# Latent attention over a prompt: value columns as the stationary operand for two heads at once, and GpSimd dividing the probabilities

## The chip, the core and the metric

The kernel runs on one core of one Trainium2 chip. The metric is the device time of one execution in microseconds (us); lower is better. A core has a matrix engine (TensorE, "PE" in the profile, with its weight loads shown apart as "PEld"), a vector engine (VectorE, "DVE"), an activation engine (ScalarE, "ACT"), a general engine (GpSimd, "POOL") and SyncE ("SP"), which only issues transfers. Each engine works through its own list of instructions in order and waits on semaphores for the others. Matrix products go from SBUF to PSUM, an accumulator memory of eight banks of 512 fp32 columns on 128 partitions.

## The reference

One decoder layer is computed for a prompt of 1024 tokens and for one new token of each of eight requests. It has dilated attention, latent attention (MLA), gates, cross attention to a memory, and a feed-forward part. The change is in the latent attention of the prompt alone:

```python
def mla_prompt(qc, rows):            # qc: 8 heads, rows: latent 256 | rotated key 32
    vals = rows[..., :MLA_KV_LORA]
    def block(b):                    # 128 queries at a time
        logits = einsum('bqhc,bkc->bhqk', qb, rows) * MLA_SCALE
        logits = where(kpos[None, :] <= t[:, None], logits, -inf)
        p = softmax(logits, axis=-1)
        return einsum('bhqk,bkc->bqhc', p, vals)
...
o_b = einsum('bshc,chv->bshv', o_lat, p['w_uv'])   # 64 value columns per head
```

Everything is fp32, and the scores are causal.

## The kernel before

The program is a sequence of stages with a barrier of all engines between them. The stage in question is the second block of `stage_mla`. It finds the queries in `qnT` and `qrT`, the normed latent rows in `rowT`, the rotated keys in `krT`, and the values of all heads, already multiplied by `w_uv`, as `vtok` (128 tokens of a key tile on the partitions, 64 columns for each head). Keys of a pair of heads are made by `keys` as a product with `w_uk`, in two halves of 512 tokens, and ScalarE copies them to `kh` (`key_copy`).

The work is cut into 64 units: 8 heads by 8 query tiles of 128 tokens. Unit (h, t) has t + 1 key tiles, so its cost grows along a head. A unit goes through these steps:

1. `score` (line 1022, TensorE): one or two products of up to 512 key columns into one of two double banks of PSUM. It waits until the unit two places before has been exponentiated (`probs`).
2. `front` (VectorE): adds the causal mask to the diagonal tile (line 1131), takes the row maximum (line 1135), and scales it by `-MLA_SCALE` (line 1136).
3. `exp` (line 1090, ScalarE): writes the unnormalised probabilities to `mla_pr`, and their sums to a column of `mla_stat`.
4. the reciprocal of the sums (line 1153, VectorE).
5. `turn` (line 1034, TensorE): transposes each 128 by 128 tile of probabilities, four into PSUM bank 4 and the others into bank 5.
6. The copies of the turned tiles to `mla_pt`: VectorE copies the first four (line 1158), ScalarE the others (line 1107).
7. `apply` (line 1046, TensorE): the turned probabilities are the weights and the 64 value columns of the head are streamed, so that the output has tokens on the partitions.
8. `normalise` (line 1143, VectorE): multiplies the 64 output columns by the reciprocal and puts them in `mla_otok`.

Units follow each other with t running inside h. TensorE's list has `score(u + 1)`, `turn(u)`, `apply(u - 1)`; VectorE's has `front(u + 1)`, the reciprocal, the copy and `normalise(u - 1)`. After the last unit TensorE turns `mla_otok` (line 1068), and VectorE and ScalarE copy it to `obT`, heads on the partitions, which the next product needs.

GpSimd has side work in this stage: it copies the queries of heads 1 to 7 to `qh` (`queries`, lines 1175 and 1177), makes the row numbers of the cache pages for the following stage, lays out the queries of that stage (lines 1192 and 1195, four rounds of 16 small copies), and at its end starts the gather of the first cache pages (line 1200, `first_rows`). None of this stands in the way of a unit, except the queries of the next head. SyncE has 24 transfers in this stage that move the cache windows to the outputs, from one place of HBM to another.

The following stage reads 32 units of cache pages by gathers from GpSimd (line 1266), and VectorE begins it by transposing the first page (line 1375).

Of the kernel before, what the change touches and what calls it, by code (L numbers as in the profile page):

```python
# [24 lines left out]
P = 128  # L25
# [599 lines left out]
def stage_mla(nc, ins, outs, top, sem, sb, ps, mats, ones, gq, gkv, latT, lat, obT, part_scr, s_copy, end_phase,  # L625
# [328 lines left out]
    with ExitStack() as st:  # L954
        HR = NOPE + ROPE
        qh = sb(st, "mla_qh", [P, 2, SEQ])
        kh = sb(st, "mla_kh", [P, 2, SEQ])
# [8 lines left out]
        qh_set, q0_set, kr_set, pool_own = sem("qh_set"), sem("q0_set"), sem("kr_set"), sem("mla_pool_own")  # L966
# [4 lines left out]
        applied, normed = sem("mla_applied"), sem("mla_normed")  # L971
        o_turned, ob_copied = sem("o_turned"), [sem("ob_copied_v"), sem("ob_copied_a")]
        tiles = [(h, t) for h in range(H) for t in range(QT)]
        N_U = len(tiles)


# [5 lines left out]
        with nc.Block() as block:  # L982
# [15 lines left out]
            def _(pe):  # L998
# [8 lines left out]
                def score(u):  # L1007
                    h, t = tiles[u]
                    if t == 0:
# [4 lines left out]
                        if h == 0:  # L1014
                            pe.wait_ge(kr_set, 3)
                    if t in (0, 4):
                        pe.wait_ge(k_copied, 4 * (h // 2) + h % 2 + (3 if t else 1))
                    if u >= 2:
                        pe.wait_ge(probs, u - 1)
                    for lo in range(0, (t + 1) * P, 512):  # L1020
                        n = min(512, (t + 1) * P - lo)
                        last = nc.tensor.matmul(ps[:, 2 * (u % 2) + lo // 512, 0:n], qh[spans[h % 2], h % 2, t * P:(t + 1) * P],
                                                kh[spans[h % 2], h % 2, lo:lo + n], start=True, stop=True)
                    last.then_inc(scored, 1)

                def turn(u):
                    t = tiles[u][1]
                    pe.wait_ge(probs, u + 1)
                    for hi in range(t // 4 + 1):
# [3 lines left out]
                        for k in range(4 * hi, min(4 * hi + 4, t + 1)):  # L1033
                            last = nc.tensor.transpose(ps[:, 4 + hi, (k - 4 * hi) * P:(k - 4 * hi + 1) * P],
                                                       pr[:, u % 2, k * P:(k + 1) * P], ident)
# [17 lines left out]
                for u, (h, t) in enumerate(tiles):  # L1053
                    if u + 1 < N_U:
                        score(u + 1)
                    turn(u)
                    if u >= 1:
                        apply(u - 1)
                    if t in (3, 7) and h % 2 and h + 1 < H:
                        keys((h + 1) // 2, t // 4)  # L1060
                apply(N_U - 1)

                for t in range(QT):
                    pe.wait_ge(normed, (H - 1) * QT + t + 1)
                    if t >= 4:
                        pe.wait_ge(ob_copied[t % 2], (t - 2) // 2)
                    for c in range(4):
                        last = nc.tensor.transpose(ps[:, t % 4, c * P:(c + 1) * P], otok[:, t, c * P:(c + 1) * P], ident)
                    last.then_inc(o_turned, 1)

            @block.scalar
            def _(act):
                def key_copy(p, half, odd):
                    act.wait_ge(k_made, 2 * p + half + 1)
                    if p:
                        act.wait_ge(scored, (2 * p - 1 + odd) * QT)
# [1821 lines left out]
```

## Time and profile before

| what | value |
|---|---|
| runs | 2304.74, 2307.99, 2309.16 us; median 2307.99 us |
| profiled execution | span 2303.0 us from its first to its last instruction; no other time of that execution is listed, and the median of the runs is 5.0 us above this span |
| TensorE busy | 2133.7 us, 93% of the span |
| VectorE, ScalarE, GpSimd busy | 1036.3, 518.8 and 83.4 us |
| mean granted TensorE clock | 0.959 |
| the stage of the change | about 577 to 778 us of the span |

The profile counts an engine as busy while an instruction of it runs. Matrix products are pipelined and overlap, so the sum of their durations is larger than the busy time. "Idle before" is time in which an engine waited, and the arrow names what ended the wait. A PE instruction count is that of passes: an fp32 product is issued as two passes, each with its own weight load, and a transpose as one.

### The profile page before, as it was taken

Reading aid. Unit: us, or ns where it says so; the run is one execution under the profiler, and the core shown is the slowest. Engines: PE = TensorE matmul, PEld = TensorE weight load, DVE = VectorE, ACT = ScalarE, POOL = GpSimd, SP = SyncE. Lnnn points to the kernel's source line nnn. Section 1 sums busy time; section 2 is a strip of 40 time slices with the busy share of each in tenths; the row PEclk is TensorE's granted clock in tenths of the full one; section 3 lists DMA queues with packets and bytes.
Section 4 is the critical chain, followed back from the end, with each engine's and each line's share of the span. In section 5 each row is a group of like instructions: output and inputs, shape, how many; then the busy total and the mean of one; then the engine's idle time right before and its main releaser. Section 6 shows DMA issues by size and latency. Waiting matters only on the chain. (4 is left out here: it accounts for less than half of the span.)

```text
span 2303.0 us, 40007 instructions
## 1 busy us (share of the span) xinstructions
PE 2133.7 (93%) x17452; PEld 1864.2 (81%) x17452; DVE 1036.3 (45%) x1338; ACT 518.8 (23%) x959; POOL 83.4 (4%) x139
## 2 busy tenths in 40 slices
PE   8999967789899889988999999789999999999998
PEld 7999945564677545557988898679999999999998
DVE  5222244644666678972222335675323323422424
ACT  4000004430434223331111223352101101101111
POOL 0000000001400011100000000000000000000000
PEclk9999977889999899998999999899999999999999
DMA  6113132020895389965211130301111111111122
GB/s 210 47 46 128 28 111 83 2 60 21 286 327 196 142 304 335 350 236 171 73 41 47 53 119 10 110 19 37 55 46 38 55 46 38 47 55 38 47 59 79
DMA packets 178911, 241.74 MB, mean 105 GB/s; under 512 B 27211, under 2 KB 165427, under 8 KB 173412
## 3 DMA queue, kind: packets, MB, share of 16 engines
q1 hardware_dynamic: 172792, 155.80, 22.0%
q0 software_dynamic: 5904, 83.95, 9.8%
q8 instruction: 94, 1.54, 0.3%
q10 hardware_dynamic: 92, 0.20, 0.0%
q14 instruction: 29, 0.24, 0.0%
HBM read 217.20 MB, written 66.72 MB: 123 GB/s over the span
## 5 line engine op out<-in xcount | busy, mean ns | idle before, releaser
L2530 PE MATMUL ps<-xn_hi,mlp_w_hi 128*128 128x344 f32 x768 | 163.3, 321 | 2.6 <-issue 2.0
L2530 PE MATMUL ps<-xn_hi,mlp_w_lo 128*128 128x344 f32 x768 | 162.4, 319 | 2.9 <-issue 2.9
L2530 PE MATMUL ps<-u_lo,mlp_w_hi 128*128 128x344 f32 x768 | 163.0, 320 | 0.0
L2530 PE MATMUL ps<-u_hi,mlp_w_hi 128*128 128x344 f32 x768 | 162.9, 320 | 0.0
L1282 PE MATMUL ps<-mla_rt,q_now 32*32 32x256 f32 x4608 | 147.3, 388 | 16.8 <-issue 9.9
L2530 PE MATMUL ps<-mlp_xn_lo,mlp_w_hi 128*128 128x344 f32 x768 | 162.8, 320 | 0.0
L2530 PE MATMUL ps<-u_hi,mlp_w_lo 128*128 128x344 f32 x768 | 162.1, 319 | 0.0
L1282 PEld LDWEIGHTS ps<-mla_rt,q_now 32*32 32x32 f32 x4608 | 86.2, 107 | 65.1 <-issue 39.8
L1375 DVE STREAM_TRANSPOSE mla_rt<-qkvT 128x1536 f32<-128x1536 f32 x72 | 124.4, 1758 | 30.5 <-DMA qkvT<-in_cache_mla,page_rows 27.8
L1693 DVE TENSOR_TENSOR hT<-hT,ps 128x1032 f32<-128x1032 f32 x28 | 34.4, 1229 | 223.9 <-PE ps L2530 223.9
L2530 PE MATMUL ps<-xn_hi,gate_w_hi 128*128 128x344 f32 x576 | 128.6, 332 | 6.5 <-DVE gates L2069 4.3
L2530 PEld LDWEIGHTS ps<-xn_hi,mlp_w_hi 128*128 128x128 f32 x768 | 128.7, 188 | 6.7 <-issue 5.6
L2530 PEld LDWEIGHTS ps<-u_lo,mlp_w_hi 128*128 128x128 f32 x768 | 130.0, 189 | 0.0
L2530 PEld LDWEIGHTS ps<-u_hi,mlp_w_hi 128*128 128x128 f32 x768 | 129.2, 188 | 0.0
L2530 PEld LDWEIGHTS ps<-xn_hi,mlp_w_lo 128*128 128x128 f32 x768 | 128.9, 188 | 0.0
L2530 PEld LDWEIGHTS ps<-mlp_xn_lo,mlp_w_hi 128*128 128x128 f32 x768 | 128.7, 188 | 0.0
L2530 PEld LDWEIGHTS ps<-u_hi,mlp_w_lo 128*128 128x128 f32 x768 | 127.9, 188 | 0.0
L2530 PE MATMUL ps<-xn_hi,win_hi 128*128 128x344 f32 x576 | 123.4, 322 | 4.1 <-DVE xn_lo L2794 4.1
L2530 PE MATMUL ps<-gates_xn_lo,gate_w_hi 128*128 128x344 f32 x576 | 123.6, 323 | 0.0
L2530 PE MATMUL ps<-xn_hi,gate_w_lo 128*128 128x344 f32 x576 | 123.2, 323 | 0.0
L2530 PE MATMUL ps<-xn_hi,win_lo 128*128 128x344 f32 x576 | 122.5, 321 | 0.0
L2530 PE MATMUL ps<-xn_lo,win_hi 128*128 128x344 f32 x576 | 122.5, 321 | 0.0
(407 smaller groups left out, 3438.4 us busy)
## 6 DMA issues: line engine op xcount, KB each, us to landing
out_s_dsa_w<-in_cache_dsa_w SPq DMA_DIRECT2D x8, 4094.0 KB, 81.7
oaT<-in_w_up SPq DMA_DIRECT2D x32, 512.0 KB, 4.1
oaT<-in_w_down SPq DMA_DIRECT2D x32, 512.0 KB, 4.0
obT<-in_w_in SPq DMA_DIRECT2D x23, 512.0 KB
gate_w<-in_w_in SPq DMA_DIRECT2D x16, 512.0 KB, 4.1
out_s_dsa_w<-in_cache_dsa_w SPq DMA_DIRECT2D x8, 1022.0 KB, 17.9
s_kv_tile<-in_cache_dsa_w SPq DMA_DIRECT2D x12, 512.0 KB, 5.3
x_scr<-qkvT SPq DMA_DIRECT2D x1, 4128.0 KB, 13.3
```

Of the source, the lines that this page charges most:

```text
L1282: last = nc.tensor.matmul(ps[32 * (JG * s + g):32 * (JG * s + g) + 32, i, 0:JN * SQ], q_now[SQ * i:SQ * i + SQ, s, c, :], rt[SQ * i:SQ * i ...
L1375: nc.vector.transpose(rt[:, k * n:(k + 1) * n], rows[v][:, :, k * n * SQ:(k + 1) * n * SQ].rearrange("p n (c f) -> p c n f", c=n)).then_in ...
L1693: nc.vector.tensor_tensor(h, h, banks(s), ALU.add).then_inc(drained[s], 1)
L2530: last = nc.tensor.matmul(out[:, t, 0:TC], w, x[:, k, t * TC:(t + 1) * TC], start=first, stop=stop)
```

## The change

The order of the units becomes: pairs of heads, then query tiles, then the two heads of the pair. `apply` is done once for a pair and a query tile. The 64 value columns of a head are now the weights, and the 128 by 128 turned probabilities are streamed; the even head uses the first 64 columns of the array and the odd head the last 64 (`tile_position`). The output has value columns on the partitions, in the layout of `obT`, and ScalarE copies it there. `mla_otok`, its transposes and its copies are gone.

The sums no longer lie on the partitions of the output. So GpSimd multiplies the probabilities by the reciprocals, in place, before they are turned, and `turn` waits for that (`normed`). The queries are multiplied by `-MLA_SCALE` when they are copied, the mask is subtracted, and the row minimum is taken, so that the step of line 1136 is gone. There are three buffers of probabilities in place of two, four of turned ones in place of two, and two sets of queries and keys. GpSimd's side work is spread among its multiplications: `queries` after units 3 and 5 of each block of 16 units, the second set of rotated keys and two clears after units 1 and 2, the page rows after unit 8, the four rounds of small copies (now `page_queries`) after units 17, 19, 21 and 23, and the gather of the first pages after the last unit.

```diff
-        pr = sb(st, "mla_pr", [P, 2, SEQ])
-        pt = sb(st, "mla_pt", [P, 2, QT, P])
-        otok = sb(st, "mla_otok", [P, QT, H * VD])
+        PRS, PTS = 3, 4
+        pr = lat_flat[:, 0:PRS * SEQ].rearrange("p (s n) -> p s n", s=PRS)
+        pt = sb(st, "mla_pt", [P, PTS, QT, P])
-        tiles = [(h, t) for h in range(H) for t in range(QT)]
+        tiles = [(2 * p + o, t) for p in range(H // 2) for t in range(QT) for o in range(2)]
+        PU = 2 * QT
...
                 def turn(u):
                     t = tiles[u][1]
-                    pe.wait_ge(probs, u + 1)
+                    pe.wait_ge(normed, u + 1)
...
-                def apply(u):
-                    h, t = tiles[u]
-                    pe.wait_ge(pt_copied[0], u + 1)
+                def apply(n):
+                    h, t = tiles[2 * n]
+                    pe.wait_ge(pt_copied[0], 2 * n + 2)
                     if t >= 4:
-                        pe.wait_ge(pt_copied[1], his(u + 1))
-                    if u >= 1:
-                        pe.wait_ge(normed, u)
+                        pe.wait_ge(pt_copied[1], his(2 * n + 2))
+                    if n:
+                        pe.wait_ge(o_copied, n)
                     for k in range(t + 1):
-                        last = nc.tensor.matmul(ps[:, 6, 0:VD], pt[:, u % 2, k, :], vtok[:, k, h * VD:(h + 1) * VD],
-                                                start=(k == 0), stop=(k == t))
+                        for o in range(2):
+                            last = nc.tensor.matmul(ps[VD * o:VD * o + VD, 6, 0:P],
+                                                    vtok[:, k, (h + o) * VD:(h + o + 1) * VD],
+                                                    pt[:, (2 * n + o) % PTS, k, :], start=(k == 0), stop=(k == t),
+                                                    tile_position=(0, VD * o), skip_group_check=True)
                     last.then_inc(applied, 1)
...
+                score(1)
+                for u in range(N_U + 2):
+                    if 1 <= u <= N_U:
+                        turn(u - 1)
+                    if u + 2 < N_U:
+                        score(u + 2)
+                    if u % 2 and u >= 3:
+                        apply((u - 3) // 2)
+                    if u % PU in (4, 10) and u // PU + 1 < H // 2:
+                        keys(u // PU + 1, 0 if u % PU == 4 else 1)
...
-                nc.scalar.activation(qh[0:NOPE, 0, :], qnT[0:NOPE, 0, 0:SEQ], ACT.Copy).then_inc(q0_set, 1)
+                nc.scalar.activation(qh[0:NOPE, 0, 0, :], qnT[0:NOPE, 0, 0:SEQ], ACT.Copy, scale=-MLA_SCALE).then_inc(q0_set, 1)
...
+                for u in range(N_U + 3):
+                    if u % 2 == 0 and u >= 4:
+                        n = (u - 4) // 2
+                        h, t = tiles[2 * n]
+                        act.wait_ge(applied, n + 1)
+                        nc.scalar.activation(obT[:, h // 2, t * P:(t + 1) * P], ps[:, 6, 0:P],
+                                             ACT.Copy).then_inc(o_copied, 1)
                     if u + 1 < N_U:
                         exp(u + 1)
...
-                    link(nc.vector.tensor_tensor(diag, diag, mats[:, C_CAUSAL:C_CAUSAL + P], ALU.add))
+                    link(nc.vector.tensor_tensor(diag, diag, mats[:, C_CAUSAL:C_CAUSAL + P], ALU.subtract))
...
-                    link(nc.vector.tensor_reduce(stat[:, u % 4, 0:1], src, AX_X, ALU.max))
-                    nc.vector.tensor_scalar(stat[:, u % 4, 1:2], stat[:, u % 4, 0:1], -MLA_SCALE, None,
-                                            ALU.mult).then_inc(maxed, 1)
+                    nc.vector.tensor_reduce(stat[:, u % 4, 0:1], src, AX_X, ALU.min).then_inc(maxed, 1)
-                def normalise(u):
-                    h, t = tiles[u]
-                    dve.wait_ge(applied, u + 1)
-                    dve.wait_ge(inverted, u + 1)
-                    nc.vector.tensor_scalar(otok[:, t, h * VD:(h + 1) * VD], ps[:, 6, 0:VD], stat[:, u % 4, 3:4], None,
-                                            ALU.mult).then_inc(normed, 1)
...
+                for u in range(N_U + 1):
                     if u + 1 < N_U:
                         front(u + 1)
+                    if u < N_U:
+                        dve.wait_ge(probs, u + 1)
+                        nc.vector.reciprocal(stat[:, u % 4, 3:4], stat[:, u % 4, 2:3]).then_inc(inverted, 1)
                     if u >= 1:
+                        nk = min(tiles[u - 1][1] + 1, 4)
+                        dve.wait_ge(turned[0], u)
+                        if (u - 1) // 2 >= 2:
+                            dve.wait_ge(applied, (u - 1) // 2 - 1)
+                        nc.vector.tensor_copy(pt[:, (u - 1) % PTS, 0:nk, :].rearrange("p k n -> p (k n)"), ps[:, 4, 0:nk * P]
+                                              ).then_inc(pt_copied[0], 1)
...
+                def normalise(u):
+                    n = (tiles[u][1] + 1) * P
+                    pool.wait_ge(inverted, u + 1)
+                    nc.gpsimd.tensor_scalar(pr[:, u % PRS, 0:n], pr[:, u % PRS, 0:n], stat[:, u % 4, 3:4], None,
+                                            ALU.mult).then_inc(normed, 1)
+                    pool.wait_ge(normed, u + 1)
...
+                for u in range(N_U):
+                    normalise(u)
+                    if u == 1:
+                        for s in range(2):
+                            nc.gpsimd.tensor_copy(kh[ropes[s], 1, s, :], krT[ropes[s], 0:SEQ]).then_inc(kr_set[1], 1)
+                            pool.wait_ge(kr_set[1], s + 1)
+                    if u == 2:
+                        nc.gpsimd.memset(kh[0:ROPE, 1, 1, :], 0.0).then_inc(kr_set[1], 1)
+                        pool.wait_ge(kr_set[1], 3)
+                        link(nc.gpsimd.memset(qh[0:ROPE, 1, 1, :], 0.0))
+                    if u % PU in (3, 5) and 2 * (u // PU + 1) < H:
+                        queries(2 * (u // PU + 1) + (u % PU - 3) // 2)
+                    if u == 8:
...
+                    if PU <= u < PU + 8 and u % 2:
+                        page_queries((u - PU) // 2)
                 pool.wait_ge(q0_set, 2)
                 pool.indirect_dma_start(first_rows[:], None, cache_rows,
```

## Rows read from the trace of the kernel before

**Rows 1.** Page: busy time of each engine, whole span.
```profile
PE 2133.7 (93%) x17452; PEld 1864.2 (81%) x17452; DVE 1036.3 (45%) x1338; ACT 518.8 (23%) x959; POOL 83.4 (4%) x139
```

**Rows 2.** Windows: length, PE, PEld, DVE, ACT, POOL busy, PE clock, DMA share, GB/s.
```profile
577.00:587.40 10.40, 6.39 (x12) 2.46 (x12) 5.56 (x10) 6.07 (x9) 6.47 (x12) 0.77 0.34 89
...
633.00:656.00 23.00, 21.68 (x143) 16.88 (x141) 16.40 (x50) 9.12 (x22) 2.06 (x2) 1.00 0.98 326
...
778.00:800.00 22.00, 15.30 (x315) 8.72 (x317) 15.37 (x15) 2.91 (x6) 2.82 (x3) 0.69 0.81 327
```

**Rows 3.** Waits in the stage, 576 to 780 us: total us, times, longest.
```profile
POOL mla_qh L1175 <- PE ps L1022: 100.9, 5, 21.3
...
DVE ps L1131 <- PE ps L1022: 38.0, 49, 2.9
...
DVE mla_otok L1143 <- PE ps L1046: 17.1, 16, 2.2
```

**Rows 4.** Groups of instructions by shape, 576 to 780 us: busy us, mean ns, idle before.
```profile
L1046 PE MATMUL ps<-qkvT,mla_pt 128*128 128x64 f32 x576 | 72.2, 271 | 0.5 <-DVE mla_otok L1143 0.5
...
L1158 DVE COPY mla_pt<-ps 128x512 f32<-128x512 f32 x40 | 27.0, 675 | 3.0 <-PE ps L1034 3.0
...
L1131 DVE TENSOR_TENSOR ps<-ps,mats 128x128 f32<-128x128 f32 x64 | 19.0, 297 | 38.0 <-PE ps L1022 38.0
L1143 DVE TENSOR_SCALAR mla_otok<-ps,mla_stat 128x64 f32<-128x64 f32 x64 | 17.7, 277 | 17.1 <-PE ps L1046 17.1
L1003 PE MATMUL ps<-qkvT 128*128 128x512 f32 x32 | 17.4, 669 | 6.2 <-PEq L693 4.9 <-ACT mla_kh L1077 1.3
...
L1153 DVE RECIPROCAL mla_stat<-mla_stat 128x1 f32<-128x1 f32 x64 | 9.8, 153 | 1.5 <-ACT mla_pr L1090 1.5
L1135 DVE TENSOR_REDUCE mla_stat<-ps 128x1 f32<-128x1024 f32 x8 | 9.8, 1225 | 0.3
...
L1090 ACT ACTIVATE mla_pr<-ps,mla_stat 128x1024 f32<-128x1024 f32 x8 | 8.9, 1113 | 18.0 <-DVE mla_stat L1136 18.0
...
L1135 DVE TENSOR_REDUCE mla_stat<-ps 128x1 f32<-128x128 f32 x8 | 2.3, 292 | 0.3
...
L1158 DVE COPY mla_pt<-ps 128x128 f32<-128x128 f32 x8 | 2.2, 274 | 0.2 <-PE ps L1034 0.2
```

**Rows 5.** Timeline of PE in the earlier dilated attention: start, us, instructions.
```profile
399.69 1.09 PE L542 MATMUL ps<-obT,arena 128*64 128x128 f32 x16 [2.33 <-ACT obT L577]
```

**Rows 6.** GpSimd's groups by shape, whole span: busy us, mean ns.
```profile
L1192 POOL COPY latT<-qkvT 32x256 f32<-32x256 f32 x32 | 12.5, 390 | 2.0
...
L1195 POOL COPY latT<-qkvT 32x8 f32<-32x8 f32 x32 | 6.1, 190 | 1.9
L863 POOL TENSOR_TENSOR oaT<-oaT,obT 128x1024 f32<-128x1024 f32 x2 | 4.7, 2350 | 55.2 <-DVE obT L894 55.2
...
L1186 POOL TENSOR_SCALAR page_rows<-page_rows 128x32 int32<-128x32 int32 x1 | 0.3, 299 | 2.9 <-DMA page_rows<-in_page_table 2.9
```

**Rows 7.** Timeline of GpSimd in the stage: start, us, instruction.
```profile
578.57 1.38 POOL L1175 COPY mla_qh<-qkvT 64x1024 f32<-64x1024 f32 x1
...
649.28 1.03 POOL L1175 COPY mla_qh<-qkvT 64x1024 f32<-64x1024 f32 x1 [21.27 <-PE ps L1022]
...
719.32 1.04 POOL L1175 COPY mla_qh<-qkvT 64x1024 f32<-64x1024 f32 x1 [21.19 <-PE ps L1022]
```

**Rows 8.** Timeline of all engines at the stage's end and after it.
```profile
767.44 1.09 PE L1034 MATMUL ps<-mats,mla_pr 128*128 128x128 f32 x8 [1.03 <-ACT mla_pr L1090]
...
770.51 1.97 PE L1046 MATMUL ps<-qkvT,mla_pt 128*128 128x64 f32 x16 [0.47 <-DVE mla_otok L1143]
...
776.02 0.60 ACT L1115 ACTIVATE obT<-ps 128x512 f32<-128x512 f32 x1 [0.28 <-PE ps L1068]
778.36 2.67 SPq L1248 DMA_DIRECT2D qkvT<-out_s_mla_rows  x8
...
789.83 3.44 DVE L1375 STREAM_TRANSPOSE mla_rt<-qkvT 128x1536 f32<-128x1536 f32 x2 [6.02 <-DMA qkvT<-in_cache_mla,page_rows]
```

More of the change, by code:

```diff
@@ L1013, in score @@
                             pe.wait_ge(qh_set, h)
-                        if h == 0:
-                            pe.wait_ge(kr_set, 3)
+                        if o == 0 and p < 2:
+                            pe.wait_ge(kr_set[p], 3)
                     if t in (0, 4):
-                        pe.wait_ge(k_copied, 4 * (h // 2) + h % 2 + (3 if t else 1))
+                        pe.wait_ge(k_copied, 4 * p + (2 if t else 0) + o + 1)
                     if u >= 2:
@@ L1021, in score @@
                         n = min(512, (t + 1) * P - lo)
-                        last = nc.tensor.matmul(ps[:, 2 * (u % 2) + lo // 512, 0:n], qh[spans[h % 2], h % 2, t * P:(t + 1) * P],
-                                                kh[spans[h % 2], h % 2, lo:lo + n], start=True, stop=True)
+                        last = nc.tensor.matmul(ps[:, 2 * (u % 2) + lo // 512, 0:n],
+                                                qh[spans[o], p % 2, o, t * P:(t + 1) * P],
+                                                kh[spans[o], p % 2, o, lo:lo + n], start=True, stop=True)
                     last.then_inc(scored, 1)
@@ L1052, in _ @@
                 score(0)
[L1053 to L1069, printed above, removed]
+                score(1)
[8 more added lines that the diff above has]
+                        keys(u // PU + 1, 0 if u % PU == 4 else 1)
             @block.scalar
@@ L1074, in key_copy @@
                     act.wait_ge(k_made, 2 * p + half + 1)
-                    if p:
-                        act.wait_ge(scored, (2 * p - 1 + odd) * QT)
-                    nc.scalar.activation(kh[parts[odd], odd, half * 512:(half + 1) * 512], ps[parts[odd], 7, :],
+                    if p >= 2:
+                        act.wait_ge(scored, (p - 1) * PU)
+                    nc.scalar.activation(kh[parts[odd], p % 2, odd, half * 512:(half + 1) * 512], ps[parts[odd], 7, :],
                                          ACT.Copy).then_inc(k_copied, 1)
@@ L1082, in exp @@
                     act.wait_ge(maxed, u + 1)
-                    if u >= 2:
-                        act.wait_ge(turned[0], u - 1)
-                        if his(u - 1):
-                            act.wait_ge(turned[1], his(u - 1))
+                    if u >= PRS:
+                        act.wait_ge(turned[0], u - PRS + 1)
+                        if his(u - PRS + 1):
+                            act.wait_ge(turned[1], his(u - PRS + 1))
                     if u >= 4:
@@ L1196, in _ @@
                                                    qrT[ROPE * (h % 4):ROPE * (h % 4) + ROPE, h // 4, SEQ:T]))
-                for h in range(2, H):
-                    queries(h)
+                nc.gpsimd.iota(sub_row[:], pattern=[[0, 1]], base=0, channel_multiplier=1).then_inc(sub_made, 1)
+                link(nc.gpsimd.memset(qh[0:ROPE, 0, 1, :], 0.0))
+                queries(1)
+                for u in range(N_U):
[11 more added lines that the diff above has]
+                    if u == 8:
+                        pool.wait_ge(sub_masked, 1)
+                        pool.wait_ge(tab_in, 16 * UNIT)
+                        link(nc.gpsimd.tensor_scalar(row_of[:], row_of[:], SUB, None, ALU.mult))
+                        link(nc.gpsimd.tensor_tensor(row_of[:], row_of[:], sub(sub_row[:, 0:1], [0, NU]), ALU.add))
+                        link(nc.gpsimd.memset(qq[:, CB - 1], 0.0))
+                    if PU <= u < PU + 8 and u % 2:
+                        page_queries((u - PU) // 2)
                 pool.wait_ge(q0_set, 2)
```

85 lines of the change are left out of this document (31 added, 54 removed).

## The prediction

> **What bounds the kernel now.** The page comes first: TensorE is busy for 93% of the span and no other engine for half of it [rows 1]. That is an average over many stages, so the stage of the change has to be read alone. Its windows show a full head with TensorE busy 21.68 of 23.00 us at a granted clock of 1.00 (the 2.4 GHz level), VectorE 16.40, ScalarE 9.12 and GpSimd 2.06 [rows 2]. The waits agree: VectorE waited 38.0 us in all for scores and 17.1 us for `apply`, and GpSimd's query copies waited 100.9 us for scores, because GpSimd had nothing else to do [rows 3]. So TensorE sets the pace, and GpSimd is the engine with room. How long a head takes is read from GpSimd, whose query copy starts once for each head: at 649.28 and, three heads later, at 719.32, that is 23.35 us a head [rows 7]. With the busy share of the window (0.943), TensorE works 22.0 us of it.
>
> The transfers of the cache windows fill the DMA engines in the stage (share 0.98 [rows 2]), but no unit waits for one.
>
> **TensorE's part.** Before, the turned probabilities are weights and 64 columns are streamed. The last `apply` has 16 passes for the 8 key tiles of one head and takes 1.97 us [rows 8]. After, 64 columns are weights and 128 columns are streamed, in two halves of the array. That form stands in the trace already, in the dilated attention (line 542: 128 by 64 weights, 128 columns streamed, two heads side by side): 16 passes for 8 pairs of key tile and head take 1.09 us [rows 5]. All `apply` is 72.2 us [rows 4]; 72.2 x 1.09 / 1.97 = 39.9, so 32.3 us go, 4.0 a head, and TensorE's work becomes 18.0 us a head. Of this the keys are 17.4 / 8 = 2.2 [rows 4] and the rest is 15.8 / 36 = 0.44 for each key tile.
>
> VectorE loses its `normalise` (17.7 us [rows 4]) and the scaling of the maximum. What is left is mask 0.30, minimum 0.29 for one key tile to 1.23 for eight (0.13 more for each), reciprocal 0.15, copy 0.27 for one to 0.68 for four or more [rows 4]. For units of one to four key tiles that is 1.02, 1.28, 1.55 and 1.82, together 5.7 us, where TensorE needs 0.44 x 10 = 4.4. So VectorE sets the pace of the short units and a head gets 1.3 us longer; half of the key work (1.1) falls among short units, where it then costs nothing. In long units TensorE leads: 3.5 us for eight key tiles against VectorE's 2.4. Half of before's 1.35 us of waiting a head I leave in (0.7), since hand-overs remain. A head comes to 18.0 + 1.3 - 1.1 + 0.7 = 18.9, say 19.0: 4.35 less than now, 34.8 us for eight heads. ScalarE gets 32 copies of 128 columns from PSUM, none longer than the 0.60 us of a copy of 512 [rows 8], four a head beside 9.12 us of work [rows 2]: hidden as long as TensorE or VectorE leads.
>
> **GpSimd's multiplication.** The trace has no fp32 multiplication by a per-partition number on GpSimd, so it is bounded from both sides. A copy, one tensor in and one out, takes 0.390 us for 256 columns [rows 6] and 1.03 for 1024 [rows 7]: 0.83 ns a column and 0.18 us fixed. A sum of two tensors takes 2.35 us for 1024 [rows 6], 2.12 ns a column. The only `TENSOR_SCALAR`, on 32 integers, takes 0.299 us [rows 6], above a copy of that size, which warns a little. The multiplication has one tensor in and one out, so I take the copy's price and keep the sum's for the range. At the copy's price eight key tiles are 1.03 us; a head is 4608 x 0.83 ns + 8 x 0.18 = 5.3 us, far under 19.
>
> What it costs is latency in a ring: score, mask, minimum, reciprocal, multiplication, turn, and the score two units later (TensorE issues `turn(u - 1)` before `score(u + 2)`). For eight key tiles, four passes as long as those of line 1003 (17.4 / 32 = 0.54 [rows 4]), 0.30, 1.23, 0.15, 1.03 and 1.09 [rows 4, 7, 8] give 6.0 us for two units, 3.0 for one, under TensorE's 3.5. At 2.35 for the multiplication it is 3.65 a unit, over 3.5.
>
> The Trainium skill, in GPSIMD Engine Reference, section Engine selection, speaks against giving GpSimd elementwise work: about half of VectorE's speed for two inputs, though roughly line-rate for one. This trace agrees on the first (2.35 us against VectorE's 1.2 for a minimum of as many columns); for the second there is a copy's 0.83 ns a column, and no multiplication. By the slower rule the time would be that of the first rival, which is worked out from rows below.
>
> **GpSimd's side work, now in the way.** While GpSimd does something else, the next multiplication waits, then `turn`, and with it all of TensorE's list behind it (`score(u + 2)`, `apply`, keys). With three buffers of probabilities, ScalarE and VectorE run on for one or two units at most.
> - The four rounds of small copies took 12.5 + 6.1 us with 2.0 + 1.9 between them [rows 6], 22.5 us in all, and were hidden behind the first units. Now they stand after units 17, 19, 21 and 23, among units of two to four key tiles. From the end of multiplication 17 to the start of 24 GpSimd has 22.5, two `queries` (four copies of 1.03, 4.1) and six multiplications (2304 columns x 0.83 ns + 6 x 0.18 = 3.0): 29.6 us. Unhindered those seven steps are 2 x (1.28 + 1.55 + 1.82) + 0.44 x 5 = 11.5, with hand-overs 12. Loss 17.6 us.
> - Six blocks of about 2.1 us (two copies of 1.03, or clears of that size) after units 1, 2, 3, 5, 35 and 37. GpSimd's free time in such a unit is about 1.2 (1.02 to 1.82 less 0.29 to 0.61). Each loses some 0.9: 5 us. Bounds 0 and 12.
> - TensorE idles in the stretch of rounds, and the granted clock falls where it idles (a mean of 0.77 and 0.69 in the windows that begin with a wait at a barrier, 1.00 in the steady one [rows 2]). In the stretch that costs nothing; after it, 1 us.
> - The first pages' gather left right after the copies of 719.32 [rows 7] and was long in when the next stage began. Now it leaves after the last multiplication, some 6 us before that stage. The second page, asked for at the start of that stage, landed at 789.83 [rows 8], some 11 us later, so the first can be up to 5 us late. But VectorE then waited 6.02 us for the second page [rows 8], and that wait takes up the delay: 0 to 5, I take 1.
>
> **The end.** From the last exponential (turn at 767.44) to the last copy (776.02 + 0.60) are 9.2 us [rows 8]. After: reciprocal 0.15, multiplication 1.03, turn 1.09, copy 0.68, `apply` of two heads 2 x 1.09, copy at most 0.60: 5.7. Gain 3.5. Negating the queries and subtracting the mask cost nothing: the same instructions with another constant, the first before any unit.
>
> **Sum.** -34.8 + 17.6 + 5 + 1 + 1 - 3.5 = -13.7 us on a span of 2303.0. The median of the runs is 5.0 above that span; I keep the distance: 2308.0 - 13.7 = 2294.
>
> **The rivals.**
> 1. GpSimd multiplies at the two-input price (slower). The ring then binds, some 0.15 a unit (9.6 us); the six multiplications in the stretch take 3.0 more; each `queries`, now two multiplications of 1024 columns, takes 2.6 more, for two heads in the stretch (5.3) and four elsewhere (10.6). Together 28.5: 2322. It decides from 1.46 ns a column on, where the sum is zero. For it: the 0.299 us row. Against it: one input. Chance 0.17, a quarter of it ending within the bound of no change.
> 2. The two halves of the array don't run at once. `apply` then takes about what it took, -34.8 shrinks to about -5, and the time is 2324. Against it: line 542 [rows 5]. Chance 0.04.
> 3. The ring, not TensorE, sets the pace of long units too, through hand-overs that I have not counted: 20.5 us a head, 12 us more, 2306, no change. For it: six hand-overs in the ring and ScalarE's list, where the output copy stands before the next exponential. Against it: 3.0 against 3.5. Chance 0.15.
> 4. The rounds are hidden after all, if the stages around them have run ahead: 2294 - 17.6 = 2276. Against it: three buffers. Chance 0.08.
>
> **How the numbers follow.** The forecast keeps 0.56. A measurement of this kernel can tell 0.2%, 4.6 us, from no change. Faster holds the forecast, rival 4 and 0.3 of rival 3: 0.68. No change: most of rival 3 and a quarter of rival 1: 0.13. Slower: 0.19. The low end takes 0.7 less waiting a head (5.6) and blocks that cost nothing (5) and a little of rival 4: 2281. The high end goes 20 us up, to 1.74 ns a column: 2314. Inside the forecast alone, 2283 to 2303.
>
> **What would show it.** Line 542's price for the new `apply`; heads at 19 us where GpSimd has no side work (units 48 to 63); GpSimd busy without a break for some 30 us around units 17 to 24, with TensorE waiting for its multiplication; a multiplication of 1024 columns at 1.03 us. The forecast is wrong if that row is above 1.7 us, if the last 16 units don't get faster, or if the rounds' stretch shows no wait.

## The result, and the profile after

| | runs | median |
|---|---|---|
| before | 2304.74 to 2314.10 us (4) | 2308.57 us |
| after | 2336.36 to 2348.65 us (4) | 2343.34 us |

The ratio is 1.0154, with an interval of 1.0127 to 1.0181: the change made the kernel slower by 35 us, where 14 us faster were predicted. The profiled execution has a span of 2346.9 us (2303.0 before). The execution profiled before is the fastest of its four and the one profiled now the slowest, so these spans lie 43.9 us apart. Nearly all of that, 43.6 us, lies in the stage of the change: from ScalarE's first query copy to the first `q_now` of the next stage it took 200.9 us before and takes 244.5 us now.

First GpSimd's groups of the changed kernel in that stage, which answer to the copies of [rows 6, 7] (line, engine, operation, shapes, count, busy us, mean ns, idle before):

```profile
L1173 POOL TENSOR_SCALAR latT<-latT,mla_stat 128x1024 f32<-128x1024 f32 x8 | 22.7, 2843 | 3.1 <-DVE mla_stat L1146 2.8
...
L1163 POOL TENSOR_SCALAR mla_qh<-qkvT 64x1024 f32<-64x1024 f32 x7 | 19.7, 2809 | 0.6
L1165 POOL TENSOR_SCALAR mla_qh<-qkvT 32x1024 f32<-32x1024 f32 x7 | 19.3, 2762 | 0.6
...
L1180 POOL COPY latT<-qkvT 32x256 f32<-32x256 f32 x32 | 12.6, 393 | 2.0
...
L1173 POOL TENSOR_SCALAR latT<-latT,mla_stat 128x128 f32<-128x128 f32 x8 | 4.8, 603 | 10.5 <-DVE mla_stat L1146 10.2
```

The multiplication (line 1173) of 1024 columns takes 2.84 us where 1.03 was predicted. From 128 to 1024 columns that is (2843 - 603) / 896 = 2.5 ns a column. The queries (lines 1163 and 1165), copies of 1.03 before, have become the same kind of instruction and take 2.8 each, with 64 or 32 partitions alike. Copies cost what they did (0.393 us for 256 columns, 0.390 before).

TensorE's groups: the new `apply` (line 1048) has the price that line 542 had promised. The turn (line 1035) waited 57.2 us for the multiplication.

```profile
L1035 PE MATMUL ps<-mats,latT 128*128 128x128 f32 x288 | 49.0, 300 | 57.2 <-POOL latT L1173 57.2
L1048 PE MATMUL ps<-mla_pt,qkvT 128*64 128x128 f32 x576 | 40.1, 285 | 0.7 <-DVE mla_pt L1152 0.7
```

The waits of the stage (total us, times, longest): before, VectorE waited for TensorE for 38.0 and 17.1 us [rows 3]. Now TensorE waits for GpSimd's multiplication, and VectorE's copy of the turned tiles waits for TensorE's turn behind it.

```profile
...
PEld ps L1035 <- POOL latT L1173: 74.7, 39, 9.3
DVE mla_pt L1152 <- PE ps L1035: 73.7, 46, 9.2
PE ps L1035 <- POOL latT L1173: 57.2, 30, 9.1
```

The windows, from the first exponential of 1024 columns of one pair of heads to that of the next (columns as in [rows 2]): the second pair, the third, and the fourth, which makes no keys for a next one.

```profile
631.16:703.81 72.65, 44.89 (x273) 27.25 (x272) 27.08 (x66) 19.98 (x52) 57.26 (x84) 0.84 0.99 328
703.81:757.21 53.40, 42.36 (x273) 26.31 (x272) 26.86 (x66) 19.87 (x52) 38.62 (x20) 0.90 0.22 75
757.21:798.27 41.06, 35.46 (x265) 22.63 (x264) 26.47 (x66) 17.85 (x48) 27.56 (x16) 1.00 0.00 1
```

Two heads took 46.7 us before (2 x 23.35). The pair with the rounds takes 72.65, the pair with two `queries` 53.40, and even the pair without side work only falls to 41.06, where GpSimd multiplies for 27.56 us. GpSimd and not TensorE is the busiest engine in the first of these windows (57.26 us against 44.89). In the first two, where TensorE waits most, its granted clock is 0.84 and 0.90, not 1.00.

The fourth pair shows the ring of the prediction. Neither engine is busy throughout: TensorE's turn waits 5.6 us in it for the multiplication, and the multiplication waits 13.3 us for VectorE's reciprocals (757.21 to 798.27 us).

```profile
POOL latT L1173 <- DVE mla_stat L1146: 13.3, 14, 1.9
...
PE ps L1035 <- POOL latT L1173: 5.6, 9, 2.1
```

GpSimd's timeline behind unit 17 (start, us) shows the stretch that the prediction put at 29.6 us:

```profile
643.64 3.56 POOL L1180 COPY latT<-qkvT 32x256 f32<-32x256 f32 x8
647.26 1.92 POOL L1183 COPY latT<-qkvT 32x8 f32<-32x8 f32 x8
649.27 1.94 POOL L1173 TENSOR_SCALAR latT<-latT,mla_stat 128x256 f32<-128x256 f32 x2
651.30 2.76 POOL L1163 TENSOR_SCALAR mla_qh<-qkvT 64x1024 f32<-64x1024 f32 x1
...
683.62 1.96 POOL L1183 COPY latT<-qkvT 32x8 f32<-32x8 f32 x8
685.67 3.86 POOL L1173 TENSOR_SCALAR latT<-latT,mla_stat 128x640 f32<-128x640 f32 x2
```

The last round ends at 685.58, 42 us after the first began, with no gap above 0.1 us between any two rows of the stretch.

The end of the stage, all engines:

```profile
807.77 1.21 POOL L1210 DMA_INDIRECT qkvT<-in_cache_mla,page_rows  x1 [0.30 <-POOL latT L1173]
...
811.35 0.28 ACT L1102 ACTIVATE obT<-ps 128x128 f32<-128x128 f32 x1 [2.10 <-PE ps L1048]
819.82 2.66 SPq L1258 DMA_DIRECT2D qkvT<-out_s_mla_rows  x8
```

The last copy ends at 811.63 and the next stage begins at 819.82, 8.2 us later (776.62 to 778.36, 1.7 us, before [rows 8]). No engine has an instruction in between. The next stage begins 12.05 us after the gather's issue.

### The profile page after: what moved, and what is told of

Read it like the earlier page. It is cut to its first block and busy times, and to the rows that moved or that the text cites. A ratio compares the mean times of both kernels' runs of the same rounds, so it can differ in the third digit from the quotient of the medians.

```text
span 2346.9 us, 39858 instructions
## 1 busy us (share of the span) xinstructions
PE 2126.9 (91%) x17420; PEld 1833.2 (78%) x17420; DVE 1014.5 (43%) x1206; ACT 523.6 (22%) x987; POOL 221.5 (9%) x207
## 5 line engine op out<-in xcount | busy, mean ns | idle before, releaser
L1292 PE MATMUL ps<-mla_rt,q_now 32*32 32x256 f32 x4608 | 145.6, 386 | 17.4 <-DVE mla_rt L1385 12.2
```

Of the source, the lines that this page charges most:

```text
L1292: last = nc.tensor.matmul(ps[32 * (JG * s + g):32 * (JG * s + g) + 32, i, 0:JN * SQ], q_now[SQ * i:SQ * i + SQ, s, c, :], rt[SQ * i:SQ * i ...
```

## The experiments

Executions differ in when the stage begins (566.7 to 578.7 us) and by up to 6.3 us behind it, whatever was changed in the stage. So the stage is compared by its own parts, read from each run's timeline as above. One execution of each kernel is profiled. It lies up to 8 us from the median of its kernel's runs, so a difference of stages can be some 10 us off the ratio: the stage of e8 is 10.2 us shorter than that of before, while its ratio of 0.9911 stands for 20 us. And where the granted clocks differ, a microsecond or two between the pairs of two kernels proves nothing, as e2 shows. In the table, "to unit 14" runs from ScalarE's first query copy to the first exponential of 1024 columns, "end" from the last pair's first such exponential to the last copy, "gap" from there to the next stage. All is in us; the ratio is to the kernel before on the same chip. (The 38.5 us that the expectations of e4 and e5 have for the last pair were cut at other marks.)

| kernel | to unit 14 | pair 2 | pair 3 | pair 4 | end | gap | stage | ratio [interval] |
|---|---|---|---|---|---|---|---|---|
| after | 55.8 | 72.65 | 53.40 | 41.06 | 13.4 | 8.2 | 244.5 | 1.0154 [1.0127, 1.0181] |
| e1 no product | 41.5 | 38.16 | 38.16 | 34.77 | 10.6 | 1.8 | 165.0 | 0.9833 [0.979, 0.9876] |
| e2 early gather | 56.3 | 74.12 | 54.89 | 42.67 | 13.4 | 1.8 | 243.1 | 1.0172 [1.0136, 1.0208] |
| e3 plain queries | 50.2 | 67.19 | 46.43 | 41.09 | 13.4 | 8.4 | 226.7 | 1.0099 [1.0063, 1.0136] |
| e4 rounds spread | 57.0 | 54.92 | 54.98 | 42.98 | 14.2 | 8.6 | 232.7 | 1.0097 [1.0064, 1.013] |
| e5 VectorE divides | 43.1 | 40.67 | 40.70 | 37.22 | 11.2 | 1.8 | 174.7 | 0.9855 [0.9827, 0.9882] |
| e6 e3 and e4 | 49.9 | 45.68 | 46.59 | 42.11 | 14.8 | 8.6 | 207.7 | 0.9994 [0.997, 1.0017] |
| e7 two tensors | 53.8 | 65.95 | 47.78 | 36.96 | 11.4 | 7.4 | 223.3 | 1.0064 [1.0041, 1.0087] |
| e8 copy, plain queries | 45.0 | 55.12 | 38.28 | 35.07 | 10.6 | 6.8 | 190.7 | 0.9911 [0.988, 0.9941] |
| e9 e7 and e3 | 44.8 | 58.82 | 40.75 | 36.94 | 11.4 | 7.4 | 200.2 | 0.9989 [0.9968, 1.001] |
| e10 e9 and e4 | 46.7 | 40.74 | 40.75 | 36.95 | 11.4 | 8.4 | 185.0 | 0.9896 [0.9852, 0.994] |
| e11 ScalarE divides | 42.8 | 40.88 | 40.88 | 38.13 | 11.7 | 1.8 | 176.2 | 0.9897 [0.9859, 0.9936] |
| e12 e10, early gather | 46.5 | 41.42 | 41.22 | 37.10 | 11.4 | 1.8 | 179.5 | 0.9898 [0.9872, 0.9924] |

**e1: the product left out.** `turn` waits for the exponentials again, and GpSimd keeps its side work. The kernel leaves out the division.

```diff
-                    pe.wait_ge(normed, u + 1)
+                    pe.wait_ge(probs, u + 1)
...
-                    normalise(u)
```

> Leaves out GpSimd's multiplication: the probabilities are not divided by their sums, and the turn waits for the exponentials. All of GpSimd's other work stays and the new apply stays. Theory A (GpSimd now stands in series with every unit: its multiplication lengthens the ring and each us of its side work is a us of the stage): the 61 us of side work leave the path, the gather of the first pages leaves early, and a pair of heads takes 35 to 37 us throughout; the time is about 2343 - 66 - 7 - 8 = 2262. Rival B (the order in pairs, the output copies in ScalarE's list or the new apply cost the time): the pairs stay above 46 us, the time stays above 2308.

It took 2264.45 us, near theory A's 2262, though the pairs are longer than its 35 to 37 us. All that the change loses hangs on the product and on what waits behind it: 79.5 us of stage, of which the gather's gap is 6.4. What is left runs at 38.16 us a pair, 19.08 a head, and its windows, of pairs 2 and 4, say why:

```profile
613.71:651.87 38.16, 37.62 (x273) 24.46 (x273) 26.29 (x66) 19.98 (x52) 25.07 (x52) 1.00 1.00 332
...
690.03:724.80 34.77, 34.23 (x265) 22.89 (x265) 25.92 (x66) 17.82 (x48) 0.00 (x0) 1.00 0.71 248
```

TensorE is busy for 37.62 of 38.16 us at a clock of 1.00, while GpSimd does 25 us of side work that nobody waits for.

**e2: the gather behind unit 38.**

> The gather of the first pages is issued after unit 38, behind the last reading of the tile that it overwrites, in place of after unit 63. Theory A (the barrier at the stage's end waits for the gather to land): from the last output copy to the next stage 1.7 us in place of 8.2, the time is 6.5 us less, 2337. Rival B (the barrier waits for something else, and only the first page is late): the 8.2 us stay, the time is 2343.

It took 2343.73 us. The gap fell from 8.2 to 1.8 us as in theory A, so the barrier does wait for the gather. It isn't GpSimd that is held up, for its next multiplication starts 1.25 us after the issue:

```profile
742.11 1.20 POOL L1211 DMA_INDIRECT qkvT<-in_cache_mla,page_rows  x1 [0.30 <-POOL latT L1173]
743.36 1.59 POOL L1173 TENSOR_SCALAR latT<-latT,mla_stat 128x512 f32<-128x512 f32 x1
```

The time did not follow; it is that of rival B. Of the 6.4 us, 5.1 were lost in the pairs (0.5 up to unit 14, then 1.5, 1.5 and 1.6), with a lower granted clock (0.77, 0.88 and 0.96 for pairs 2 to 4, where after has 0.84, 0.90 and 1.00). The first two of these stretches lie ahead of the gather, so it can't have caused that part. Why the clock was lower in this execution stays open.

**e3: the queries as plain copies.** The scale moves to the copies of the keys.

```diff
...
-                    link(nc.gpsimd.tensor_scalar(qh[parts[o], p % 2, o, :],
-                                                 qnT[NOPE * o:NOPE * o + NOPE, p, 0:SEQ], -MLA_SCALE, None, ALU.mult))
+                    link(nc.gpsimd.tensor_copy(qh[parts[o], p % 2, o, :],
+                                               qnT[NOPE * o:NOPE * o + NOPE, p, 0:SEQ]))
...
```

> GpSimd copies the queries (1.03 us for 1024 columns) in place of multiplying them (2.76); the scale goes to the copies of the keys on ScalarE and of the rotated keys on VectorE. Theory A (side work is paid one for one): six heads x 2 x 1.73 = 20.8 us less, 2322. Rival B (the pace of those stretches comes from TensorE's lower clock or from the short units themselves): less than 10 us, above 2333.

It took 2328.0 us; the stage is 17.8 us shorter. Pair 3 holds two `queries` and gains 7.0. Their four instructions got 4 x (2.79 - 1.08) = 6.8 us shorter, so there the price of side work is paid one for one, as in theory A. Pair 2 gains 5.5 by four such instructions. The twelve for heads 2 to 7 together got 20.5 us shorter, and the stage 17.8. Their row now:

```profile
L1164 POOL COPY mla_qh<-qkvT 64x1024 f32<-64x1024 f32 x7 | 7.6, 1082 | 0.4
```

**e4: the small copies, two by two behind the 32 long units.**

```diff
...
-                    if PU <= u < PU + 8 and u % 2:
-                        page_queries((u - PU) // 2)
+                    if tiles[u][1] >= 4:
+                        page_queries(his(u))
```

> The 64 small copies of the four rounds stand two by two (0.6 us) behind the 32 units of five to eight key tiles, in place of four rounds of 5.5 us behind units 17 to 23. Theory A in its strict form (every us of GpSimd's side work costs a us wherever it stands, because its multiplication sits in the ring): no change, 2343. Theory B (what costs is a block longer than GpSimd's free time in a unit, and in the last pair GpSimd is idle 11.5 of 38.5 us): the 22 us of rounds are hidden, 2321.

It took 2326.57 us, nearer to theory B. Pair 2 lost its rounds and 17.7 us. The stretch up to unit 14 and pairs 3 and 4, which now hold some of the copies, became 1.2 to 1.9 us longer, and the end 0.8: 5.5 us in all. Not all of that need be the copies': pair 4 takes 42.98 us at a granted clock of 0.96, and in e2, with no copies in it, 42.67 at the same 0.96. Either way the copies cost far less spread out than as four blocks among short units, even with GpSimd this slow.

**e5: VectorE divides**, right behind its reciprocal.

```diff
...
                         nc.vector.reciprocal(stat[:, u % 4, 3:4], stat[:, u % 4, 2:3]).then_inc(inverted, 1)
+                        dve.wait_ge(inverted, u + 1)
+                        n = (tiles[u][1] + 1) * P
+                        nc.vector.tensor_scalar(pr[:, u % PRS, 0:n], pr[:, u % PRS, 0:n], stat[:, u % 4, 3:4], None,
+                                                ALU.mult).then_inc(normed, 1)
...
```

GpSimd's product is gone.

> The multiplication by the reciprocal is done by VectorE, in place, right behind the reciprocal; GpSimd keeps only the queries and the small copies. Theory A (only GpSimd's price and its place behind the side work made the change slow; the last pair of heads, 38.45 us, shows the pace of the rest): VectorE was busy 23.8 of those 38.5 us, and 16 multiplications of a pair, 9,216 columns at 1.07 ns (its maximum over 1024 columns took 1.22 us) with 0.06 each, add about 10.8 us, 34.6 in all, still under 38.5. Each pair takes 39 to 42 us, the stage 168 to 180 us, the kernel 2265 to 2280 us on this chip. Theory B (VectorE's order becomes the bound, since the multiplication stands between the maximum of one unit and the copy of another): pairs of 45 to 48 us, as without the change, and 2290 to 2305 us.

It took 2274.37 us, faster than both kernels, with time and stage in theory A's ranges. The second pair's window, and the row of the multiplication:

```profile
616.57:657.24 40.67, 37.93 (x274) 24.40 (x273) 34.86 (x81) 20.08 (x52) 26.73 (x52) 1.00 0.99 330
```

```profile
L1149 DVE TENSOR_SCALAR latT<-latT,mla_stat 128x1024 f32<-128x1024 f32 x8 | 7.3, 916 | 0.3
```

The same instruction takes 0.92 us on VectorE, under the 1.07 ns a column that the expectation allowed, against 2.84 on GpSimd. VectorE is busy for 34.9 us of a pair and the pair is 2.5 us longer than without any product: TensorE, busy for 37.93 of 40.67 us, is still the bound.

The Trainium skill, in VectorE: DVE Perf Modes, section "The perf-mode tier table", puts an fp32 `tensor_scalar` within SBUF at twice the rate of a reduction. The trace agrees in direction: 0.92 us against 1.22 for the minimum of as many columns.

**e6: e3 and e4 together.**

> GpSimd still multiplies, but the queries are plain copies (e3) and the small copies go two by two behind the long units (e4). Theory A (the two savings add, -17.8 and -11.8 us of stage): stage near 215 us, time 2310 to 2316 us on this chip, still not faster than before. Theory B (with both, GpSimd has enough slack in a pair that what remains is hidden): pairs of 40 to 42 us, stage near 190 us, 2285 to 2295 us. Theory C (they overlap, since either made room for the other's work): stage near 225 us, about 2325 us.

It took 2302.33 us, the time of before, between theories A and B. The stage shrank by 36.8 us, more than the two savings together (29.6). But pairs 2 and 3 stay at 45.7 and 46.6: with a product of 2.84 us GpSimd works 36 us in a pair. From pair 2 to pair 4 (616.59 to 750.97 us) TensorE's turn waits 20.2 us for the multiplication, and the multiplication 23.8 us for reciprocals, so the ring through it still sets the pace.

**e7: the product in the form with two tensors.** The reciprocal is read as a second tensor with stride 0.

```diff
-                    nc.gpsimd.tensor_scalar(pr[:, u % PRS, 0:n], pr[:, u % PRS, 0:n], stat[:, u % 4, 3:4], None,
-                                            ALU.mult).then_inc(normed, 1)
+                    nc.gpsimd.tensor_tensor(pr[:, u % PRS, 0:n], pr[:, u % PRS, 0:n], sub(stat[:, u % 4, 3:4], [0, n]),
+                                            ALU.mult).then_inc(normed, 1)
```

> The multiplication stays on GpSimd, but as an operation with two tensors: the reciprocal is read as a second tensor of stride 0 along the row, in place of a scalar per partition. The queries keep the scalar form. Theory A (2.5 to 2.8 ns a column is the price of the form with a scalar, and the two-tensor form costs 2.12 ns a column plus about 0.18 us, as in its row of before): 1024 columns take 2.35 us instead of 2.84, and the three pairs with side work gain about 3.5 us each; stage near 234 us, time about 10 us under the changed kernel's. Theory B (the price comes from the fp32 data or from sharing memory with VectorE, whatever the form): 2.8 us again and no change.

It took 2320.63 us, 21 us of stage less than after, twice what theory A expected. GpSimd's groups:

```profile
L1163 POOL TENSOR_SCALAR mla_qh<-qkvT 64x1024 f32<-64x1024 f32 x7 | 19.7, 2811 | 0.6
...
L1173 POOL TENSOR_TENSOR latT<-latT,mla_stat 128x1024 f32<-128x1024 f32 x8 | 15.2, 1894 | 3.5 <-DVE mla_stat L1146 3.2
...
L1173 POOL TENSOR_TENSOR latT<-latT,mla_stat 128x128 f32<-128x128 f32 x8 | 3.2, 401 | 13.9 <-DVE mla_stat L1146 13.9
```

The same product costs 1.89 us in this form: (1894 - 401) / 896 = 1.67 ns a column. So with the same fp32 data in the same place the form of the instruction alone moves the price from 2.84 to 1.89 us, against theory B. Why the form with one tensor is the slower one, no run shows.

**e8: a copy in the product's place, and plain queries.** GpSimd's large instructions then cost what the prediction had assumed, and the probabilities stay undivided.

```diff
-                    nc.gpsimd.tensor_scalar(pr[:, u % PRS, 0:n], pr[:, u % PRS, 0:n], stat[:, u % 4, 3:4], None,
-                                            ALU.mult).then_inc(normed, 1)
+                    nc.gpsimd.tensor_copy(pr[:, u % PRS, 0:n], pr[:, u % PRS, 0:n]).then_inc(normed, 1)
```

> GpSimd copies the probabilities onto themselves where it multiplied them (so they stay undivided), and the queries are plain copies with the scale moved to the copies of the keys, as in e3. So every large instruction of GpSimd has the price that the prediction gave it, 0.83 ns a column. Theory A (that price was the one term that failed in the loop; rounds and side blocks cost what the prediction said, 17.6 and 5 us): 1024 columns take about 1.03 us, the stage takes 4 x 38.4 plus 23 plus the 24 us around them, near 200 us, and the kernel 2295 to 2302 us. Theory B (with a cheap product GpSimd catches up between the blocks, so that they cost less than one for one): stage 180 to 190 us and 2275 to 2288 us. Theory C (blocks of side work are paid one for one whatever the product costs, 22 for the rounds and some 20 for the rest): 2305 us or more.

It took 2287.09 us, in the range of theory B, with a stage of 190.7. The prediction's sum for this case is 200.9 - 13.7 = 187.2. Its row, and the windows of pairs 2 and 3:

```profile
L1173 POOL COPY latT<-latT 128x1024 f32<-128x1024 f32 x8 | 8.3, 1041 | 8.6 <-DVE mla_stat L1147 8.6
```

```profile
623.63:678.75 55.12, 42.89 (x273) 26.79 (x273) 26.93 (x66) 20.09 (x52) 33.34 (x84) 0.88 1.00 332
678.75:717.03 38.28, 37.62 (x273) 24.43 (x273) 26.33 (x66) 19.97 (x52) 14.80 (x20) 1.00 0.97 325
```

With the price put right, the loop goes as the prediction had it: 19.1 us a head, two `queries` for 0.1, rounds for 55.12 - 38.16 = 17.0. These are theory A's prices for the rounds. Its 200 us of stage were too long because it put 24 us around the four pairs, where e1 has 165.0 - 4 x 38.16 = 12.4. For the blocks of `queries` theory B was right: at this price GpSimd catches up.

**e9: the two-tensor product with plain queries.**

> GpSimd multiplies in the two-tensor form (1.89 us for 1024 columns in e7) and the queries are plain copies (e3); the small copies stay in four rounds. Theory A (what the stage loses is set by the price of the product and of the queries together, and grows about evenly between e8, 43 us of copies and a stage of 190.7, and e3, 110 us of products and a stage of 226.7): 73 us of products give a stage near 207 us and a ratio to before near 0.998. Theory B (the product is under the slack, as TensorE sets the pace at 38.2 us a pair and products take 18.4 of it, so that only blocks count): stage near 195 us and a ratio near 0.993.

It took 2297.05 us, with a stage of 200.2: no different from before, as theory A had it for the time, though the stage fell further than it said.

**e10: e9 with the small copies spread out.**

> As e9, and the small copies go two by two behind the long units (e4). GpSimd then has 18.4 us of products and about 12 us of other work in a pair of heads. Theory A (30 us under TensorE's 38.2, blocks of at most 2.2 us: nearly all hidden): pairs of 38.5 to 41 us, stage near 183 us, ratio to before 0.985 to 0.99. Theory B (a block of 2 us still stops the ring, at whatever load): pairs of 43 us, stage near 198 us, ratio 0.994 or more.

It took 2276.27 us. Theory A's price for the pairs holds, 40.74 and 40.75, the same as pair 3 of e9 without any small copies:

```profile
616.37:657.11 40.74, 38.25 (x273) 24.31 (x273) 26.71 (x66) 19.98 (x52) 27.07 (x36) 1.00 1.00 332
657.11:697.86 40.75, 38.26 (x273) 24.31 (x273) 26.72 (x66) 19.98 (x53) 27.10 (x36) 1.00 0.99 326
```

At this price they are hidden in the long units of these pairs. Against e9, the stretch up to unit 14 is 1.9 us longer and the gap 1.0, since the last copies stand ahead of the gather. So what cost 18.1 us in pair 2 of e9 costs 2.9 at most. The stage took 2 us more than expected, with a gap of 8.4 at the barrier.

**e11: ScalarE divides**, behind the next exponential.

```diff
...
+                        nc.scalar.activation(pr[:, u % PRS, 0:n], pr[:, u % PRS, 0:n], ACT.Copy,
+                                             scale=stat[:, u % 4, 3:4]).then_inc(normed, 1)
...
```

> ScalarE multiplies, behind the exponential of the next unit, with the reciprocal as its scale; GpSimd keeps queries and small copies. Theory A (TensorE sets the pace once nothing else stands in the way; ScalarE was busy 19.5 of 38.2 us in a pair, and 9,216 columns at about 1.03 ns with 0.05 each add some 10, so 30 in all): pairs of 38.2 to 39.5 us, stage 166 to 171 us, ratio 0.983 to 0.985, a little under that of e5. Theory B (the product waits behind the exponential, and the copy of the upper half of probabilities behind the product, so the round from score to turn grows): pairs of 41 to 44 us, ratio 0.986 to 0.993.

It took 2277.29 us with pairs of 40.88, between the theories; the ratio is in theory B's range. The product of 1024 columns took 1.17 us there.

```profile
L1109 ACT ACTIVATE latT<-latT,mla_stat 128x1024 f32<-128x1024 f32 x8 | 9.3, 1166 | 0.0
```

**e12: e10 with the gather behind unit 50**, and the small copies behind the 24 long units of the first three pairs.

> As e10 (two-tensor product on GpSimd, plain queries, small copies spread out), but the 64 small copies go behind the 24 long units of the first three pairs, and the first page is gathered behind unit 50, so that its 12 us of flight end inside the last pair. Theory A (the barrier waits for the gather to land, and in e10 that cost 754.64 - 745.95 - 0.28 = 8.4 us, against 1.8 in e5): the gap falls to about 1.8 us, stage near 178.5, ratio to before 0.985 to 0.987. Theory B (as in e2, what the barrier gives back is lost again in the pairs): pairs of 42 us and more, stage 183 to 186, ratio 0.989 to 0.991.

It took 2281.03 us. In the stage theory A holds: the gap fell from 8.4 to 1.8 us and the stage by 5.5, to 179.5. The ratio, 0.9898, lies in theory B's range. It can't be told from that of e10 (0.9896), whose interval of 0.4% each way is wider than the saving; and the execution profiled here is the fastest of its six, 8 us under their median.

## Why the prediction was wrong, by its own steps

**The step that failed** is the price of the multiplication: "one tensor in and one out, so I take the copy's price", 0.83 ns a column. It is 2.5, and the bound from the other side, 2.12 from a sum of two tensors, didn't hold it either. The prediction had called a row above 1.7 us a sign of being wrong; the row is 2.84. GpSimd's form with one tensor and one number is the slowest of those measured (2.84 us for 1024 columns, 2.35 for a sum of two tensors, 1.89 for the product with two tensors, 1.04 for a copy). The only row of before with that form, 0.299 us for 32 integers, was called a warning and then outweighed. With the 0.18 us fixed of a copy it would have given an estimate of (0.299 - 0.18) / 32 = 3.7 ns a column: the slow side, but not the price. The fp32 rows have 2.5 ns a column and 0.28 us fixed (0.603 - 128 x 2.5 ns), which for 32 columns would be 0.36 us.

**The same step a second time**, less visibly: "negating the queries ... cost nothing: the same instructions with another constant." They were copies and became that form. At 2.8 us instead of 1.08 they cost 17.8 us of stage (e3).

What the two cost together is shown by putting the prices in one after the other:

| from, to | stage | step |
|---|---|---|
| e8, copies throughout | 190.7 | |
| e9, product at 1.89 | 200.2 | +9.5 |
| e3, product at 2.84 | 226.7 | +26.5 |
| after, queries at 2.8 too | 244.5 | +17.8 |

That is 53.8 of the 57.3 us between the predicted stage and the measured one; the other 3.5 are those of e8, where the gather alone cost 4 more than predicted. (The medians miss by less, 2343 against 2294, because the execution profiled is the slowest of its kernel.) The step from 1.89 to 2.84 is the steepest. This fits the reason that the prediction gave for its first rival: the ring through the multiplication, 6.0 us for two long units at a product of 1.03, becomes 7.8 at 2.84, 3.9 a unit against TensorE's 3.5. Pair 4, with no side work, is 6.3 us longer than without a product (41.06 against 34.77), and TensorE's turn waits 5.6 us in it for GpSimd. GpSimd then has little reserve to catch up behind any block. In pair 3 of after, the 11.1 us of queries and these 6.3 add to 17.4; 15.2 were lost.

**The first rival** had the mechanism and the side. Its price was too low: 2322 at 2.35 us for both instructions. Its break-even, 1.46 ns a column for both, no run tests: e9 shows no change with 1.67 for the product and a copy's price for the queries.

**The other terms**, tested in e8 and e1:
- A head at 19.0 us: 19.08 in e1 and 19.14 in e8. `apply` at 39.9 us: 40.1.
- Rounds 17.6: 17.0 in e8. Their place costs this, since e10 hides nearly all of the same copies. The fourth rival, that they are hidden where the change puts them, is out.
- Side blocks 5: 45.0 - 41.5 = 3.5 ahead of unit 14 and 0.1 in pair 3.
- The late gather 1: 5.0 in e8 (gap 6.8 against 1.8) and 6.4 in after. The prediction looked at the next stage's first wait; but the barrier between the stages waits for the gather itself (e2, e12).
- The end, 3.5 gained: from the last exponential's end to the last copy's 9.2 us before, by the prediction's reading, and 6.9 in e8 (755.74 to 762.66), 2.3 gained.
- The clock, 1 us behind the rounds: 0.88 in pair 2 of e8 and 1.00 in pair 3, which is 0.1 us longer than in e1, so next to nothing there. In after it is 0.90 in pair 3 as well. What that cost was not measured apart; the table above includes it.
- The second rival (array halves not concurrent) is out by the 40.1 us of `apply`. The third is out for cheap products: with a TensorE busy for 37.62 of 38.16 us hand-overs cost almost nothing (e1; 37.62 of 38.28 in pair 3 of e8).
- The chances: by its own parts, slower comes to 0.17 and no change to 0.15, not 0.19 and 0.13. Nothing hangs on it.

The idea behind the change is sound and was put on the wrong engine or in the wrong form: with the division on VectorE (e5) the kernel is 1.45% faster than before. On GpSimd, with a two-tensor product, plain queries and the copies spread out (e10), it is 1.0% faster.

## What to carry to other kernels

Price an instruction by a row of its own form on its own engine, and where there is none, don't take the number of inputs for the form: the kind with fewer inputs was the slower one here. When an engine enters a ring, everything else that it does becomes a wait of the ring, so put its long side work beside long steps and check again what each piece costs, above all pieces that look unchanged. A transfer started late in a stage lengthened the wait at the barrier here, whoever needed its data, though the kernel's time did not show the saving of some 6 us when it started early (e2, e12).

## What the runs showed of the hardware that was not expected

- GpSimd's fp32 `TENSOR_SCALAR` takes 2.8 us for 1024 columns with a number for each partition (128 partitions) and with a constant (64 or 32 partitions) alike. The Trainium skill, in GPSIMD Engine Reference, section Engine selection, calls one-input work there roughly line-rate. Copies bear that out (1.04 us), this form doesn't, and the measurement decides.
- A two-tensor product took 1.89 us for 1024 columns with one operand of stride 0, and a sum of two full tensors 2.35 [rows 6].
- The division of 1024 columns by a number for each partition took 0.92 us on VectorE and 1.17 on ScalarE.
- The barrier waited for a gather in flight, and with the gather issued earlier it did not (gaps of 1.8 us in e2 and e12): 12.05 us from its issue in after, 11.9 in e8 (757.50 to 769.38), 11.2 in e10 (743.46 to 754.64).
